# Attention q and k turned by VectorE in 32x32 blocks instead of by TensorE, in a two-layer decoder trunk

## The reference, cut to what matters

```python
def mla_branch(c_q, c_kv, k_r, ...):
    q = (rms_norm(c_q, q_lat_g) @ w_uq).reshape(B, S, 16, 96)
    kv = (rms_norm(c_kv, kv_lat_g) @ w_ukv).reshape(B, S, 16, 64 + 64)
    k_nope, v = kv[..., :64], kv[..., 64:]
    k = jnp.concatenate([k_nope, broadcast(k_r)], axis=-1)          # 64 + 32 = 96 per head
    q, k = rms_norm(q, q_norm_g), rms_norm(k, k_norm_g)
    q, k = rope_on_last_32(q), rope_on_last_32(k)
    return causal_block_attention(q, k, v)                          # softmax(q k^T / sqrt(96)) v, 16 heads

for l in range(2):
    z = rms_norm(x, mix_norm_g[l]) @ w_in[l]                        # 1024 x 4896
    y_a = gmlp_branch(...) @ gm_w_proj[l]
    y_b = mla_branch(...) @ mla_w_proj[l]
    x = x + (sigmoid(g_a) * y_a + sigmoid(g_b) * y_b) @ w_out[l]
    x = x + (dense SwiGLU if l == 0 else top-2-of-8 SwiGLU experts)(rms_norm(x, ffn_norm_g[l]))
```

## Time and profile before

| | |
|---|---|
| timed runs | 1434.69, 1435.66, 1436.26 us; median 1435.66 |
| the profiled execution's own time | 1435.21 us |
| its span in the profile | 1433.4 us (1.8 us lie around it) |
| PE busy | 1424.1 us, 99% |
| DVE busy | 1143.1 us, 80% |
| ACT busy | 960.6 us, 67% |
| GpSimd (POOL) busy | 45.3 us, 3% |
| mean DMA rate | 290 GB/s over the span |
| mean granted TensorE clock | 0.999 |

### The profile page before, as it was taken

The page is one execution under the profiler, slowest core; times in us unless marked ns, Lnnn a source line. Parts: engine busy times, 40 slices in busy tenths (PEclk is TensorE's granted clock), DMA queues, the critical chain, the costliest instruction groups (busy, mean ns, idle before and its releaser), DMA issues.

```text
span 1433.4 us, 19210 instructions
## 1 busy us (share of the span) xinstructions
PE 1424.1 (99%) x6747; PEld 1178.6 (82%) x6747; DVE 1143.1 (80%) x1160; ACT 960.6 (67%) x1003; POOL 45.3 (3%) x54
## 2 busy tenths in 40 slices
...
PEclk9999999999999999999999999999999999999999
...
GB/s 338 162 236 118 119 157 305 332 177 178 159 214 187 149 234 118 136 159 276 290 352 414 410 359 411 380 386 409 366 402 380 380 412 372 382 386 413 372 397 161
DMA packets 163268, 415.14 MB, mean 290 GB/s; under 512 B 15420, under 2 KB 43960, under 8 KB 163176
## 3 DMA queue, kind: packets, MB, share of 16 engines
...
## 4 chain that ended last, share of the span: by engine, by line
PE 96%; ACT 2%; DVE 2%; issue 0%; POOL 0%; DVEq 0%; ACTq 0%; POOLq 0%
PE ps L552 88%; PE ps L1109 1%; PE ps L829 1%; PE ps L972 1%; PE ps L951 1%; PE ps L873 1%; PE ps L959 1%; ACT w_hi L507 1%; ACT qk_t L1252 1%; PE ps L938 0%; PE ps L907 0%; PE ps L950 0%; ACT prob L1377 0%; ACT sq L1377 0%; PE ps L846 0%
## 5 line engine op out<-in xcount | busy, mean ns | idle before, releaser
L512 DVE TENSOR_TENSOR w_lo<-raw,w_hi 128x2048 fp32r<-128x2048 f32 (+3 forms) x240 | 500.9, 2105 | 139.2 <-ACT w_hi L507 136.5
L507 ACT ACTIVATE w_hi<-raw 128x2048 fp32r<-128x2048 f32 (+3 forms) x240 | 421.9, 1769 | 187.2 <-PE ps L552 171.5
L552 PE MATMUL ps<-w_hi,act_hi 128*128 128x512 f32 (+1 forms) x1264 | 333.8, 392 | 0.1
L552 PE MATMUL ps<-w_hi,act_lo 128*128 128x512 f32 (+1 forms) x1264 | 331.3, 388 | 0.0
L552 PE MATMUL ps<-w_lo,act_hi 128*128 128x512 f32 (+1 forms) x1264 | 327.4, 387 | 0.0
L552 PEld LDWEIGHTS ps<-w_lo,act_hi 128*128 128x128 f32 x1264 | 235.6, 188 | 48.1
L552 PEld LDWEIGHTS ps<-w_hi,act_lo 128*128 128x128 f32 x1264 | 234.9, 188 | 47.8 <-DVE act_lo L1621 0.2
L552 PEld LDWEIGHTS ps<-w_hi,act_hi 128*128 128x128 f32 x1264 | 232.3, 188 | 46.0 <-ACT act_hi L1252 0.5
L512 DVE TENSOR_TENSOR w_lo<-raw_more,w_hi 128x2048 fp32r<-128x2048 f32 (+1 forms) x96 | 201.9, 2111 | 30.3 <-ACT w_hi L507 30.2
L507 ACT ACTIVATE w_hi<-raw_more 128x2048 fp32r<-128x2048 f32 (+1 forms) x96 | 170.0, 1775 | 55.4 <-PE ps L552 54.4
L512 DVE TENSOR_TENSOR w_lo<-raw_low,w_hi 128x2048 fp32r<-128x2048 f32 (+1 forms) x64 | 137.6, 2156 | 11.2 <-ACT w_hi L507 10.7
...
## 6 DMA issues: line engine op xcount, KB each, us to landing
raw<-in_moe_w_gu SPq DMA_DIRECT2D x128, 512.0 KB, 9.3
raw_more<-in_moe_w_down SPq DMA_DIRECT2D x80, 512.0 KB, 7.4
raw<-in_w_in SPq DMA_DIRECT2D x72, 512.0 KB, 4.7
raw_low<-in_moe_w_gu SPq DMA_DIRECT2D x64, 512.0 KB, 10.6
raw_more<-in_moe_w_gu SPq DMA_DIRECT2D x64, 512.0 KB, 10.8
...
raw<-in_moe_w_down SPq DMA_DIRECT2D x48, 512.0 KB, 7.1
raw<-in_dense_w_gu SPq DMA_DIRECT2D x44, 512.0 KB, 5.0
```

Of the source, the lines that this page charges most:

```text
L507: nc.scalar.activation(w_hi[:, self.split_slot(j), 0:n], self.raw(j)[:, 0:n], ACT.Copy).then_inc(self.hi, 1)
L512: nc.vector.tensor_tensor(w_lo[:, c, 0:n], self.raw(j)[:, 0:n], w_hi[:, c, 0:n].bitcast(F32), ALU.subtract).then_inc(self.lo, 1)
L552: return nc.tensor.matmul(dst, a, b, start=start and n == 0, stop=stop and n == 2)
```

## The change

q and k are no longer turned by PE. (1) `qb` and `kb` are laid out in groups of 32 features (`[P, TT, 3, H, 32]`); the strip copies of q become three copies of 160 or 192 columns a token tile instead of one, and the squares and sums run over the new layout. (2) GpSimd issues DMAs that move 32x32 blocks from one set of partitions to another within SBUF (`move_heads`): 12 DMAs for q (128 KB each), 12 for each half of k (64 KB each), 36 per layer. (3) DVE then transposes all the 32x32 blocks in place, one instruction of 96x2048 for each half of q and of k, four per layer (`blocks`). (4) ACT scales q by `qk_gain` into `q_first`, `q_second` (two copies of 96x1024 directly behind the first half's turn) and `q_last` (one of 96x2048); k's turned blocks are read by the scores where they are. (5) The steps `q_rope` move from behind ga(0,0) and ga(0,4) to behind uq(2) and ukv(0), ahead of `head_sums` of q's second half; the squares of that half get a step `head_squares` of their own on ACT ahead of the ropes. (6) `k_scale` of both halves moves ahead: behind ukv(3) and behind ga(0,0); with ga(0,0) come also q's first turn and its scaling. `head_sums` of k moves into `then`, behind the strip's copy and ahead of the `w_hi` copy of the chunk three ahead. (7) The first half of k's blocks lies in the fourth `raw` buffer, which is lent for it: from u(0) to ga(1) (ten chunks) the ring has three buffers.

The diff, cut to what the prediction speaks of:

```diff
+        if what == "u" or (what, j) in (("gb", 1), ("pa", 0), ("ga", 1)):
+            keys_in.setdefault(l, []).append(len(chunks) - 1)
...
-        mul(l, "uq", 2, 0, [evac("uq", 2)])
+        mul(l, "uq", 2, 0, [evac("uq", 2), ("head_squares", l, "q", 1), ("q_rope", l, 0)])
+        mul(l, "ukv", 0, 0, [("q_rope", l, 1), evac("ukv", 0)])
         plan.append(("head_sums", l, "q", 1))
-        mul(l, "ukv", 0, 0, [evac("ukv", 0)])
         mul(l, "ukv", 1, 0, [evac("ukv", 1)])
-        plan.append(("head_sums", l, "k", 0))
-        mul(l, "ukv", 2, 0, [evac("ukv", 2)])
-        mul(l, "ukv", 3, 0, [evac("ukv", 3)])
-        plan.append(("head_sums", l, "k", 1))
-        mul(l, "ga", 0, 0, [("mix_tokens", l, 0)])
-        plan.append(("q_rope", l, 0))
+        mul(l, "ukv", 2, 0, [evac("ukv", 2), ("head_sums", l, "k", 0)])
+        mul(l, "ukv", 3, 0, [evac("ukv", 3), ("head_sums", l, "k", 1), ("k_scale", l, 0)])
+        mul(l, "ga", 0, 0, [("mix_tokens", l, 0), ("k_scale", l, 1), ("blocks", l, "q", 0)])
         mul(l, "ga", 0, 4, [("mix_tokens", l, 1), evac("ga", 0)])
-        plan.append(("q_rope", l, 1))
         mul(l, "u", 0)
-        plan.append(("k_scale", l, 0))
+        plan.append(("blocks", l, "k", 0))
         mul(l, "u", 0, 4, [("u_arg", l, 0), ("split", l, len(chunks)), ("u_gelu", l, 0)], split=False)
-        mul(l, "u", 1, 0, [("branch", l, 0), *slot(1, exps=False)], inside=[(4, turn(0))], split=False)
-        mul(l, "u", 1, 4, [("u_arg", l, 1), *slot(2)], split=False,
-            inside=[(2, ("a_turns", l, 0)), (2, ("softmax", l, 0)), (5, turn(1)), (5, split())])
+        mul(l, "u", 1, 0, [("branch", l, 0), *slot(1, exps=False)], split=False)
+        mul(l, "u", 1, 4, [("u_square", l, 1), *slot(2, exps=False), ("u_arg", l, 1), ("blocks", l, "q", 1), ("softmax", l, 1), ("last_q", l, "q", 1)],
+            split=False,
+            inside=[(2, ("a_turns", l, 0)), (2, ("softmax", l, 0)), (5, split())])
...
+                def move_heads(to, src, heads, moved):
+                    for b in range(4):
+                        for g in range(DG):
+                            pool.dma_start(to[32 * g:32 * g + 32, b:TT * 4:4, :, :], src[32 * b:32 * b + 32, :, g, heads, :]
+                                           ).then_inc(moved, 16)
+
+                pool.wait_ge(q_ready, TT * (l + 1))
+                move_heads(q_blocks, qb, slice(0, H), q_moved)
+                pool.wait_ge(lo_done, lent_read[l] + 1)
+                pool.wait_ge(k_ready, 2 * l + 1)
+                move_heads(k_blocks[0], kb, slice(0, 8), k_moved[0])
+                pool.wait_ge(k_ready, 2 * l + 2)
+                pool.wait_ge(q_moved, 16 * 4 * DG * (l + 1))
+                move_heads(k_blocks[1], kb, slice(8, H), k_moved[1])
...
+                    dve.wait_ge(head_squares, counts["heads"] + 1 + t)
+                    rope(qb[:, t, DG - 1, :, 0:HR], qb[:, t, DG - 1, :, HR:DR], c1, n2, c2, n1, s1, s2, q_ready)
...
+                    nc.vector.transpose(part, part).then_inc(done, 1)
...
-                elif kind == "qk_turns":
-                    pair = step[2]
...
-                    for hh in range(2):
-                        bank = turn_bank(b0 + hh)
-                        for q in range(4):
-                            src = (qb, kb)[q // 2]
-                            mm = nc.tensor.transpose(bank[0:DQ, q * P:(q + 1) * P], src[:, q % 2, 2 * pair + hh, :], ident)
-                        mm.then_inc(turn_done, 1)
```

More of the change, by code:

```diff
@@ L268, in decoder_trunk @@
     N0 = len(chunks)
+    slot_of, use_of, user_before, users = [], [], [], [[] for _ in range(RAW)]
+    for n in range(N0):
+        i = min(range(RAW - any(n in c for c in keys_in.values())), key=lambda i: users[i][-1] if users[i] else i - RAW)
+        user_before.append(users[i][-1] if users[i] else None)
+        use_of.append(len(users[i]))
+        users[i].append(n)
+        slot_of.append(i)
+    last_users = sorted((u[-1], i) for i, u in enumerate(users))
+    keys_over = {min(n for n in users[-1] if n > keys_in[l][-1]): l for l in range(L)}
+    lent_read = [max(n for n in users[-1] if n < keys_in[l][0]) for l in range(L)]
     assert N0 % SPLIT == 0 and PER_EXPERT % SPLIT == 0 and PER_EXPERT % RAW_MOE == 0
@@ L483, in split_slot, with wait_slot @@
                 return (self.n0 + j) % SPLIT
-            def load(self, sp, e, j, pieces):
+            def wait_slot(self, sp, e, j):
                 r = len(self.slots)
@@ L562, in turns_in @@
             return {"norm_turns": 2, "latent_turns": 2 - step[2] if step[0] == "latent_turns" else 0, "spatial_weights": 2, "mix_tokens": 2, "merged_turns": 2,
-                    "a_turns": 2, "qk_turns": 2, "values": 1, "prob_turns": 2, "hidden_turn": 1, "down": 1 - (step[0] == "down" and step[5] > 0)}.get(step[0], 0)
+                    "a_turns": 2, "values": 1, "prob_turns": 2, "hidden_turn": 1, "down": 1 - (step[0] == "down" and step[5] > 0)}.get(step[0], 0)
         def routed(step):
@@ L1339, in _ @@
                     turn_hi_parts(b0, hid_hi, 2 * step[2], 1.0)
-                elif kind == "head_sums":
+                elif kind == "head_squares" or kind == "head_sums" and step[2:] != ("q", 1):
                     hf = step[3]
@@ L1806, in _ @@
                     ks = k_sum[:, :, heads].rearrange("p t (h o) -> p t h o", o=1)
[L1807 to L1809 removed]
+                    for g in range(DG - 1):
+                        k = kb[:, :, g, heads, :]
+                        tt(k, k, ks.to_broadcast([P, TT, 8, 32]), ALU.mult)
+                    tt(kb[:, :, DG - 1, heads, :], kr[:].rearrange("p t (o n) -> p t o n", o=1).to_broadcast([P, TT, 8, DR]),
                        ks.to_broadcast([P, TT, 8, DR]), ALU.mult).then_inc(k_ready, 1)
+                elif kind == "blocks":
+                    half = step[3]
+                    if step[2] == "q":
+                        dve.wait_ge(q_moved, 16 * 4 * DG * (l + 1))
+                        part, done = q_blocks[0:DQ, :, 8 * half:8 * half + 8, :].rearrange("p b h i -> p b (h i)"), q_turned
+                    else:
+                        dve.wait_ge(k_moved[half], 16 * 4 * DG * (l + 1))
+                        part, done = k_blocks[half][0:DQ].rearrange("p b h i -> p (b h i)"), k_turned
+                    nc.vector.transpose(part, part).then_inc(done, 1)
                 elif kind == "branch":
```

165 lines of the change are left out of this document (103 added, 62 removed).

## The result

The changed kernel takes 1438.83 us (median of 17 runs, 1437.86 to 1439.60), the one before 1435.55 (17 runs, 1434.63 to 1436.26). The ratio is 1.0023, with a 95% interval of 1.0015 to 1.0030: slower by 3.3 us, or 0.23%. The prediction was 1440 us, in a range of 1427 to 1448. The profiled execution took 1439.60 us for a span of 1437.9; it is the slowest of the 17, so its rows show up to 0.8 us more loss than the median has.

What follows compares the result with a forecast made beforehand. PE was taken to bound every stage. Per layer, new waits of 10.0 us less 0.45 of old waits and 7.15 of turns, taken as +2.2, brought the profiled 1435.2 to 1439.6, forecast as 1440 us, range 1427 to 1448.

Steps and rivals of the forecast that it cites:

- What leaves PE: Attention: PE's turns go, 0.89 us a pair, 14.3 us in all, 7.15 per layer; scores reading k in pieces cost nothing.
- The new instructions: DVE turns at 2.2 us each (1.1 to 2.3), four per layer; ACT scaling at 2.0 for q's pair, 1.95 for the last.
- Rows and chunks in time: Block DMAs, 6.4 us to issue twelve, and chunk loads land just in time, hidden even at the upper bound, costing nothing.
- DVE's queue: From the first rope at 79.5, DVE has no idle time; `w_lo` of ga(0,0) written at 92.5, q's turn ends at 107.6.
- third pass of ga(0,0): PE starts it at 91.9 but `w_lo` is written at 92.5: first wait, 0.7 us per layer.
- u(0,4): ACT's `w_hi` copy stands behind q's scaling, which waits for q's turn: second wait of PE, 2.8 us per layer.
- `a_turns` 0: PE needs DVE's `branch` at 125.6, written at 128.8: third large wait, 3.2 us per layer.
- `prob_turns` 1: Its second half needs the PSUM bank freed by pair 0's values copy, behind q's scaling and tanh: about 1.8 us.
- the rest (`prob_turns` 2): The following places, `a_turns` 1 and `prob_turns` 2 and 5, add waits of about 1.1 us per layer.
- The sum: Waits 10.0 less old waits 0.45 less turns 7.15, taken as +2.2 us per layer, +4.4 in all; likeliest case 1435 to 1446.
- TensorE's clock: Falls to 1.2 GHz behind PE's new waits: 2 to 4 us each, four 8 to 16, about 1451; chance 0.16 with late landings.
- the gain without new waits: Rival: turns leave PE and nothing new waits, 1420.5 to 1422; chance 0.23 for any gain of over 3 us.

Runs made afterwards that it cites:

- run 12: Run 3 with eight identity transposes on PE ahead of each pair's scores, 128 in all: 1435.40 us, ratio 1.0001 to the kernel before.
- run 7: Changed kernel with DVE's four turns per layer cut to half of their columns: 1433.30 us, ratio 0.9986 to the kernel before.
- run 6: Changed kernel with each of the 36 block DMAs per layer followed by a second one to spare DRAM: 1439.01 us, ratio 1.0027 to the kernel before.
- run 3: Run 2's order plus k's two scalings one step later, q's second turn and its scaling re-placed by due time: 1423.69 us, ratio 0.9917 to the kernel before.
- run 11: Changed kernel with PE's waits at u(0,4) and `a_turns` 0 filled by 20 identity transposes each, the first into the scores' idle bank: 1438.34 us.
- run 1: Changed kernel with q's first turn and its scaling copies moved behind the split of one more chunk: 1439.62 us, ratio 1.0027 to the kernel before.
- run 2: Run 1 with q's scaling copies and k's first turn behind the splits of both u(0,4) and u(1,0): 1428.47 us, ratio 0.9951 to the kernel before.
- run 4: Kernel before with 48 of PE's 64 turns per layer left out, copies kept: 1429.58 us, ratio 0.9957 to the kernel before.
- run 5: Changed kernel with 20 identity transposes ahead of u(0,4) and of `a_turns` 0; the first filling waited for its own PSUM bank: 1443.49 us, ratio 1.0064.
- run 8: Changed kernel with k's first squares and sums back ahead of the copies emptying ukv's third strip: 1438.88 us, ratio 1.0028 to the kernel before.
- run 9: Run 3 with k's first squares and sums back ahead of the copies emptying ukv's third strip: 1431.72 us, ratio 0.9977 to the kernel before.
- run 10: Run 3 with four small moves more (chunk 15's split, u's second gelu, `softmax` 2 and 5): 1422.05 us, ratio 0.9907 to the kernel before.

## Why the prediction was right, step by step

**What leaves PE**, 0.89 us a pair and 14.3 in all: right (0.88 in the rows of run 12). The scores with k in pieces of 32 cost nothing more: those of pair 1 take 1.31 us from 136.95 to 138.26, as they took before from 128.60 to 129.91.

**The new instructions**: a turn lasts 2.30 us, at the upper bound, and costs 2.22 from start to start (120.81 to 123.03), against 2.2. q's two scaling copies took 2.09 (107.98 to 110.07), against 2.0. What the turns are worth at half the length was priced at 3.3 us per layer; run 7 gave 2.8.

**Rows and chunks in time**: right for PE, with no margin for twice as many (run 6). GpSimd issued at 0.53 to 0.54 us each here too (6.45 and 6.38 for twelve). The Trainium skill (SBUF — State Buffer, section "Two separate sides") says that certain VectorE instructions keep GpSimd from writing descriptors; in this trace DVE was busy all through q's dozen with subtractions, sums and short scalar steps, and the issues took no longer. Chunks did land after ACT was ready for them, by 0.45 us at 119.76, and in run 3 by 4.23 ahead of the `w_hi` of u(0,4), and PE waited for none of these.

**DVE's queue**: the first rope was forecast for 79.5 and started at 79.52; `w_lo` of ga(0,0) was forecast written at 92.5, and was at 92.75; q's turn at 107.6, and was at 107.94. From that rope to the end of the turn DVE waited for nothing.

**The waits.** The idle times in brackets are 0.15 to 0.25 us less than what a wait costs in the distances of starts, since groups that follow each other without a wait overlap in the rows. The prediction reckoned in starts, so the cost is taken from distances of starts, less those of the same matmuls without a wait. At `a_turns` 0 of layer 1, for one, it is 560.11 less 555.47, 4.64 us, where the kernel before needs 1.58 (548.90 to 550.48).

| place | forecast | layer 0 | layer 1 |
|---|---|---|---|
| third pass of ga(0,0) | 0.7 | 1.1 | 1.1 |
| u(0,4) | 2.8 | 2.8 | 2.8 |
| scores of pair 0 | 0.4 | 0.2 | 0.2 |
| `a_turns` 0 | 3.2 | 3.0 | 3.1 |
| `prob_turns` 1 | 1.8 | 0.3 | 1.5 |
| the rest (`prob_turns` 2) | 1.1 | 0.7 | 0.7 |
| sum | 10.0 | 8.2 | 9.4 |

The places and the engines waited for are the ones forecast. The last two terms, which the prediction states without a working, came out too large, and the first too small. Behind `prob_turns` 1 stands the chain that was named: q's second turn on DVE, its scaling and the tanh on ACT, and then the copy and DVE's subtraction that free the bank.

**The sum**: +2.2 us per layer was forecast. The last stage of the attention (`merged_turns` 0) starts in the kernel before and in the changed kernel at:

```profile
218.64 1.03 PE L829 MATMUL ps<-consts,vbuf 128*128 128x128 f32 x8
...
646.41 1.03 PE L829 MATMUL ps<-consts,vbuf 128*128 128x128 f32 x8
```

```profile
221.83 1.03 PE L894 MATMUL ps<-consts,vbuf 128*128 128x128 f32 x8
...
651.27 1.03 PE L894 MATMUL ps<-consts,vbuf 128*128 128x128 f32 x8
```

That is +3.2 for layer 0 and +1.7 for layer 1. For layer 1 the table gives +1.8 (9.4 less 0.4 of an old wait and 7.15 of turns). Layer 0 has 8.2 us of waits and a fall that cost 2.9: +3.5 by the same sum, against the measured +3.2. Without a fall it was +1.6 there (run 11: 220.27). The medians' +3.3 lies 1.1 under the forecast's +4.4.

**How much of it is luck.** The forecast is the difference of two terms of 7 to 10 us, and to meet it within 1.2 us took errors that cancel: `prob_turns` 1 and the rest were 0.7 too large in layer 1, the third pass 0.4 too small. In layer 0 the waits alone were 1.8 us too large. That the total still exceeded the forecast there is due to a fall that its likeliest case had left out.

**TensorE's clock**: the forecast left it out of the likeliest case and priced a fall at 2 to 4 us. One came in the profiled execution, at one of four long stands, and cost 2.9 us at its place. The Trainium skill (TensorE: Matmul & The Clock Gate, section "Why this matters for your kernels") warns of gaps between bursts, and the traces agree that falls come at gaps, but not at each: in the profiled executions of runs 1 to 9 and of the changed kernel PE stood 22 times in the attention for 1.9 to 3.5 us, and at 10 of these the clock fell; where there were only stands of up to 1.3 us (runs 2, 3 and 10) it never did. The net cost of the falls in the changed kernel is 0.5 us by the medians of run 11, and 1.6 by the rows of runs 6 and 11.

**The rivals**: the gain without new waits (1420.5 to 1422) was real, but belonged to another order; run 10 reaches 1422.05. The condition named for it, q's first turn ended before 104.5, was wrong: run 3 ends it at 110.1 and has most of the gain. What decided was not when the turn ended but what stood behind it on ACT.
